# Hybrid decoder block: load order at the ways into gate and up and into down, and where residual pieces and the last weighting stand

## Chip, cores, metric

One core of a Trainium2 chip. The metric is the device time of one execution in microseconds, the median of three runs.

## The reference

The input is `x`, 2048 tokens of 1024 features in float32. The block computes:

```
u    = rmsnorm(x, ln1_g)
proj = u @ w_in                      # a_q a_f a_i a_g (512 columns each), b_q 512, b_k 128, b_v 128
y_a  = hgrn2_mixer(...)              # gated linear recurrence, 4 heads, chunks of 64 tokens
y_b  = swa_sink_attention(...)       # 8 query heads on 2 key heads, window 128, sinks, ALiBi
h    = x + concat(y_a, y_b) @ w_out
u    = rmsnorm(h, ln2_g)
h    = h + (silu(u @ w_gate) * (u @ w_up)) @ w_down      # 1024 -> 2816 -> 1024
out  = rmsnorm(h, final_g)
```

## The kernel before

Every product is made in three matmuls: each operand is split into a high part that TensorE multiplies in its reduced float32 form (made by ScalarE as a copy) and the remainder (made by VectorE as a subtraction), and high × high, high × remainder and remainder × high are added up in PSUM.

The tokens are worked in four blocks of 512. A first phase (`slots` and `out_b`, called for each block `it`) makes the input projection, both mixers and the output projection. The FFN then runs over two pairs of blocks, `p` = 0 and 1: `ffn(p)` makes gate and up, `down(p)` the last product. Both use a scheme with seven block products in place of eight. Its operands on the token side are named B11, B21, T2, T1, T3, B22, T4 (L69); T1 to T4 are differences that VectorE makes with `combine`, the B's are plain. Each is loaded by `load_operand` in four pieces of 256 KB from `u_scr`, split by `op_hi` (ScalarE) and `op_lo` (VectorE, 128 x 2048). The products of one weight group `g` run in the order A11, A12, S2, S1, S3, S4, A22 with the operands B11, B21, T2, T1, T3, B22, T4. Weights of a group come as two halves of 512 KB (`load_ffn`), four of the seven factors are sums that GpSimd makes in `ffn_sums`, and `ffn_hi`/`ffn_lo` split them.

`down(p)` runs over 77 rows `rr` = 11 `q` + `j`. A row is one 256-row slice step: a weight half row and an activation tile, 256 KB each, loaded by `load_row` into one of four ring places (`rr` mod 4), split by `row_hi` and `row_lo` (128 x 1024), and used by 12 matmuls for four token tiles. `load_row(rr)` waits until row `rr` - 4 is done (`s_row`); rows 1 to 3 of a pair wait for other things since their ring places share memory with buffers of `ffn`. For each of the seven `q`, VectorE adds the finished banks to the residual tiles `res` (`residual(p, q - 1, j)`, at `j` = 0 to 3 of the next `q`). The residual itself is loaded from `ht_scr` piece by piece by `load_res`; the list `PIECES` and the dictionary `pieces` in SP's `down` say behind which row's load each piece is issued. VectorE's loop in `down` is: for each `rr`, `row_lo(rr + 2)`, then the additions, then the final norm's steps.

All engines work through an order that is written out by hand; semaphores do the rest. SP issues all DMAs, so that a load whose semaphore is not met holds back all later ones. What the change and the prediction touch:

- SP: `mixers` (L807 and on, the last block's branch), the order of stores and loads in `ffn` (L848 and on), `load_row` (L730), `load_res` (L758), the dictionary `pieces` in `down` (L898 and on).
- ScalarE: `out_b` and `ffn`, the places of `op_hi(0, T4)` and `op_hi(0, B22)`; `out_square` makes the sums of squares for the final norm.
- VectorE: `residual` (L2269), `last_gain` (L2293: the right half of the last pair's second block times `final_g`, ahead of the norm factor), `out_scale`, `down`.

A load of the first weights waits in `load_ffn` for `s_group` at `NSB * UNITS - 2`, since the buffer shares memory with a weight unit of the output projection. The addition that opens the first block product waits for all its pieces at once:

```
if q in BEGINS + (2, 6) and q != 1 and b == 0:
    dve.wait_ge(s_ht[m ^ half], 128 * p + 64 * (m + 1))
```

where every piece adds 16 to its semaphore, and BEGINS is (0, 1, 3).

Of the kernel before, what the change touches and what calls it, by code (L numbers as in the profile page):

```python
# [42 lines left out]
TB = T // P  # L43
# [36 lines left out]
A11, A12, S2, S1, S3, S4, A22 = range(PRODUCTS)  # L80
B11, B21, T2, T1, T3, B22, T4 = range(PRODUCTS)
# [12 lines left out]
PIECES = (("r", 0), "T3", "T1", ("r", 2), "T2", ("r", 1), "T4", "B11", "B21", "B22", ("r", 3))  # L94
COMBINE_AT = {27: 0, 37: 1, 39: 2, 48: 3}
SPLIT_AT = {50: "B11", 52: "T2", 54: "T1", 59: "T3", 61: "B21", 63: "T4", 65: "B22"}
T_LOAD = 9
U_LAST = ((5, 6), (6, 3), (6, 6), (7, 3))

# [36 lines left out]
def block_program(nc, x, ln1_g, w_in, lb_logits, hgrn_norm_g, attn_sinks, attn_norm_g, w_out, ln2_g,  # L136
# [14 lines left out]
    NPAIR = NSB // 2  # L151
    NJ = KF // 2
# [22 lines left out]
    with ExitStack() as ctx:  # L175
# [325 lines left out]
        s_sst = sem("s_sst")  # L501
# [87 lines left out]
        def _(sp):  # L589
# [140 lines left out]
            def load_row(p, rr):  # L730

                q, j = divmod(rr, NJ)
                if rr >= CRING:
                    sp.wait_ge(s_row, p * NR + rr - CRING + 1)
                elif rr == 0 and p == 0:
                    wait_u_stored(sp, NSB - 1)
                elif rr == 1:
                    sp.wait_ge(s_flo, NQ * (p + 1))
                elif rr == 2:
                    sp.wait_ge(s_blk, 3 * NG * (p + 1))  # L740
                    sp.wait_ge(s_u, (NSB - 1) * TB + 2 * TB)
                elif rr == 3:
                    sp.wait_ge(s_c21[1], NJ * (p + 1))
                    sp.wait_ge(s_sst, 48 * (NJ * (p + 1) - 1))
                ring = RING[rr % CRING][2]
                combined, k, half = WEIGHT_HALF[q]
                if combined:
                    sp.wait_ge(s_ts, 16 * NJ)
                sp.dma_start(ring[:, 0, :], (t_scr if combined else w_down_k)[2 * j + k, :, half * T:(half + 1) * T]
                             ).then_inc(s_ring[rr % CRING], 16)  # L750
                done = p * NJ + (j + 1 if q == 0 else NJ)
                if q in (0, 1, 4, 6):
                    sp.wait_ge(s_ast[{0: 0, 1: 3, 4: 2, 6: 1}[q]], 16 * done)
                else:
                    sp.wait_ge(s_sst, 48 * done)
                sp.dma_start(ring[:, 1, :], a_scr[p, q, j, :, :]).then_inc(s_ring[rr % CRING], 16)
# [50 lines left out]
            def mixers(it):  # L807
                last = it + 1 == NSB
                for n in range(2, IN_GROUPS):
                    load_split(it, n)  # L810
                    if n < 2 + TB:
                        store_h(it - 1, n - 2)
                    if n == G2_LOAD:
                        load_g2(it)
                    if n == X_LOAD and not last:
                        for b in range(2):
                            sp.wait_ge(s_ptr0, (it + 1) * 2 * TB)
                            load_x(it + 1, b, x_next[b])
                    if n == X_LOAD_2 and not last:
                        for b in range(2, TB):  # L820
                            sp.wait_ge(s_u, it * TB)
                            load_x(it + 1, b, x_next[b])
                    if n == X_LOAD and last:
                        for b in range(2):
                            load_rows(it, b)
                for n in range(OUT_A, OUT_B):
                    if n > OUT_A:
                        store_u(it - 1, n - OUT_A - 1)
                    if last and n != OUT_A + 1:
                        load_operand(0, {OUT_A: T3, OUT_A + 2: T1, OUT_A + 3: T2}[n])  # L830
                    load_split(it, n)
                for c in range(4):
                    for what, n in ((("u", 3), ("r", 0), ("r", 1), ("u", 4)), (("u", 5), ("r", 2), ("u", 6)),
                                    (("u", 7), ("r", 3)), ())[c]:
                        if what == "u":
                            store_u(it - 1, n)
                        elif not last or n >= 2:
                            load_rows(it, n)
                    load_split(it, OUT_B + c)
                    if last:  # L840
                        load_operand(0, (B11, B21, T4, B22)[c])
                if last:
                    load_ffn(0, 0)
                else:
                    load_split(it + 1, 0)
                    load_split(it + 1, 1)

            def ffn(p):  # L848
# [5 lines left out]
                for g in range(NG):  # L854
# [11 lines left out]
                    if g % 2 == 0:  # L866
                        if 0 < g < NG - 2:
                            load_ffn(p, g + 2)
                        if p == 0 and 0 <= g - T_LOAD < NJ:
                            load_t(g - T_LOAD)  # L870
                    else:
                        last = j == NJ - 1
                        store_a(p, j, 0)
                        if last:
                            load_row(p, 0)
                        else:
                            load_ffn(p, g + 2)
                        if p == 0 and 0 <= g - T_LOAD < NJ:
                            load_t(g - T_LOAD)
                        if last:  # L880
                            load_row(p, 1)
                        store_a(p, j, 1)
                        if last:
                            load_row(p, 2)
                            load_row(p, 3)
                        store_s(p, j, 0)
                        store_s(p, j, 1)
                        if last:
                            load_row(p, 4)
                        store_a(p, j, 2)  # L890
                        store_a(p, j, 3)
                        store_s(p, j, 2)
# [5 lines left out]
            def down(p):  # L898
                pieces = {}
                for i in range(TB * len(PIECES)):  # L900
                    pieces[(6, 7, 8, 10)[i] if i < TB else 4 + i * 29 // 20] = (PIECES[i // TB], i % TB)
                assert len(pieces) == TB * len(PIECES)
                for rr in range(CRING + 1, NR):
                    load_row(p, rr)
# [435 lines left out]
        def _(act):  # L1340
# [221 lines left out]
            def out_b(it):  # L1562
# [31 lines left out]

                if not following:
                    ffn_hi(0, 1)
                    ffn_hi(0, 2)


# [43 lines left out]
            def ffn(p):  # L1643
                for g in range(NG):
                    G, j = NG * p + g, NJ * p + g // 2
                    x, y, z = banks_of(p, g)
                    for o in range(PRODUCTS):
# [27 lines left out]
                                    act.wait_ge(s_sst, 48 * j)  # L1675
                                A(gq[3][:, :], x[:, :], ACT.Silu).then_inc(s_c21[0], 1)
                        if p == 0 and g == 0 and o == A11:
                            op_hi(0, T4)
                        if p == 0 and g == 0 and o == A12:
                            op_hi(0, B22)  # L1680
                        if p == 0 and g in (1, 2) and o in (S1, S4):
                            h_square(NSB - 1, 2 * g - 2 + (o == S4))
# [103 lines left out]
        def _(dve):  # L1786
# [518 lines left out]
            def down(p):  # L2305
                for rr in range(NR):
# [2 lines left out]
                        row_lo(p, rr + 2)  # L2309
                    if q and j < TB:  # L2310
                        residual(p, q - 1, j)
                    if p + 1 == NPAIR and q == 6 and TB <= j < 2 * TB:
                        last_gain(p, j - TB)
                    if q == 6 and j == TB + 1:
                        out_sums(p, 0)
                    if q == 6 and j == TB + 2:
# [236 lines left out]
```

## Time and profile before

| | us |
|---|---|
| median of three runs | 2177.64 (2177.31 to 2179.43) |
| the profiled execution, device time | 2177.87 |
| its span | 2175.8 |
| TensorE matmul busy | 2151.5 (99%) |
| VectorE busy | 1309.5 (60%) |
| ScalarE busy | 892.6 (41%) |
| GpSimd busy | 444.1 (20%) |
| 16 DMA engines, share of the span | 53.9% |

The page gives the busy time of each engine, a strip of 40 slices of the span with the clock granted to TensorE, and groups of instructions with the idle time ahead of them and what ended it. A wait matters where it is TensorE that waits. The timeline shows single instructions: start, duration, engine, line, output and inputs, and in brackets the idle time before and what ended it.

In the trace of before, the first phase ends and `ffn(0)` begins near 894 us, `down(0)` near 1322, `ffn(1)` near 1535, `down(1)` near 1954; the last row is done near 2166.

### The profile page before, as it was taken

What the parts mean: (1) busy time and instruction counts of PE and PEld (TensorE: products, weight loads), DVE (VectorE), ACT (ScalarE), POOL (GpSimd) and SP (SyncE); (2) the same over time, 40 slices, a digit from 0 to 9 for tenths busy, and PEclk for the clock granted to TensorE, in tenths of its full rate; (3) what the DMA queues carried; (4) which work ended last, traced back from release to release, by engine and by line L of the source; (5) the groups of instructions that cost most, each with busy time, mean ns of one, the idle gap of its engine ahead of it and who ended that gap; (6) DMA issues with size and microseconds to landing.
All of it is one profiled execution on the core that took longest, in us unless ns stands there. A gap on an engine that the chain in (4) does not pass through costs nothing.

```text
span 2175.8 us, 29163 instructions
## 1 busy us (share of the span) xinstructions
PE 2151.5 (99%) x10836; PEld 1792.6 (82%) x10836; DVE 1309.5 (60%) x2046; ACT 892.6 (41%) x1692; POOL 444.1 (20%) x393
## 2 busy tenths in 40 slices
PE   8999999999999999999999999999999999999998
PEld 7888888888888888788888887888888888887886
DVE  5776466446644665666576765567755556554556
ACT  5543443334332433444333333346433333333444
POOL 2331023102310231322332230001232233210000
PEclk9999999999999999999999999999999999999999
DMA  7665744664466437543265556787432323237666
GB/s 244 228 254 204 261 165 155 195 217 166 154 198 223 165 136 231 214 139 127 98 217 208 209 202 227 260 271 249 170 106 102 105 89 121 92 99 245 223 208 222
DMA packets 215740, 402.49 MB, mean 185 GB/s; under 512 B 16944, under 2 KB 100912, under 8 KB 211760
## 3 DMA queue, kind: packets, MB, share of 16 engines
q1 hardware_dynamic: 215600, 400.63, 53.9%
q8 instruction: 87, 1.43, 0.3%
q14 instruction: 53, 0.43, 0.1%
HBM read 292.04 MB, written 108.53 MB: 184 GB/s over the span
## 4 chain that ended last, share of the span: by engine, by line
PE 93%; DVE 3%; DMA 2%; ACT 1%; issue 1%; SPq 1%; POOL 0%; DVEq 0%; ACTq 0%; POOLq 0%
PE M L1268 10%; PE M L1269 10%; PE M L1270 10%; PE M L960 7%; PE M L962 7%; PE M L961 7%; PE M L1293 3%; PE M L1294 3%; PE M L1295 3%; PE X L1270 3%; PE X L1269 3%; PE X L1268 3%; PE X L1294 3%; PE X L1295 3%; PE X L1293 3%; PE M L1085 2%
## 5 line engine op out<-in xcount | busy, mean ns | idle before, releaser
L2267 DVE TENSOR_TENSOR ring_lo<-ring_raw,ring_hi 128x1024 fp32r<-128x1024 f32 x154 | 189.6, 1231 | 165.3 <-ACT ring_hi L1701 164.8
L1701 ACT ACTIVATE ring_hi<-ring_raw 128x1024 fp32r<-128x1024 f32 x154 | 163.2, 1060 | 231.6 <-DMA ring_raw<-a_scr 228.3
L1268 PE MATMUL M<-t_hi,wu_hi 128*128 128x512 f32 x616 | 240.2, 390 | 0.2
L1270 PE MATMUL M<-t_hi,wu_lo 128*128 128x512 f32 x616 | 239.9, 390 | 0.0
L1269 PE MATMUL M<-t_lo,wu_hi 128*128 128x512 f32 x616 | 239.7, 389 | 0.0
L960 PE MATMUL M<-uhi,split 128*128 128x512 f32 (+1 forms) x528 | 207.7, 393 | 2.9 <-DVE ulo L1837 2.9
L962 PE MATMUL M<-uhi,split 128*128 128x512 f32 (+1 forms) x528 | 202.8, 384 | 0.0
L961 PE MATMUL M<-ulo,split 128*128 128x512 f32 (+1 forms) x528 | 202.4, 383 | 0.0
L2153 DVE TENSOR_TENSOR wu_lo<-fraw,wu_hi 128x512 fp32r<-128x512 f32 x132 | 123.3, 942 | 122.5 <-ACT wu_hi L1641 122.2
L2447 POOL TENSOR_TENSOR pr<-pr,rd 128x512 f32<-128x512 f32 x64 | 73.2, 1143 | 454.1 <-DVE rd L1848 454.1
L2516 POOL TENSOR_TENSOR fs<-fraw 128x512 f32<-128x512 f32 x44 | 62.7, 1424 | 446.0 <-DMA fraw<-in_w_gate_dram 209.0
L1268 PEld LDWEIGHTS M<-t_hi,wu_hi 128*128 128x128 f32 x616 | 115.6, 188 | 25.0 <-DVE wu_lo L2153 1.0
L1269 PEld LDWEIGHTS M<-t_lo,wu_hi 128*128 128x128 f32 x616 | 115.8, 188 | 23.9
L1270 PEld LDWEIGHTS M<-t_hi,wu_lo 128*128 128x128 f32 x616 | 115.6, 188 | 24.1
L2522 POOL TENSOR_TENSOR fraw<-fraw,fs 128x512 f32<-128x512 f32 x44 | 57.1, 1297 | 369.5 <-DVE wl_lo L2153 369.4
L1293 PE MATMUL M<-ring_hi 128*128 128x512 f32 x308 | 121.0, 393 | 3.2 <-DVE ring_lo L2267 3.2
L1294 PE MATMUL M<-ring_lo,ring_hi 128*128 128x512 f32 x308 | 119.9, 389 | 0.0
L1295 PE MATMUL M<-ring_hi,ring_lo 128*128 128x512 f32 x308 | 119.9, 389 | 0.0
L1293 PE MATMUL X<-ring_hi 128*128 128x512 f32 x308 | 119.9, 389 | 0.0
L1295 PE MATMUL X<-ring_hi,ring_lo 128*128 128x512 f32 x308 | 119.8, 389 | 0.0
L1294 PE MATMUL X<-ring_lo,ring_hi 128*128 128x512 f32 x308 | 119.8, 389 | 0.0
L960 PEld LDWEIGHTS M<-uhi,split 128*128 128x128 f32 x528 | 99.2, 188 | 25.0 <-issue 6.5
(301 smaller groups left out, 5024.6 us busy)
## 6 DMA issues: line engine op xcount, KB each, us to landing
split<-w_scr SPq DMA_DIRECT2D x60, 1024.0 KB, 5.4
ring_raw<-a_scr SPq DMA_DIRECT2D x154, 256.0 KB, 3.6
w_scr<-split SPq DMA_DIRECT2D x30, 1024.0 KB, 6.3
split_next<-w_scr SPq DMA_DIRECT2D x30, 1024.0 KB, 5.5
fraw<-in_w_gate_dram SPq DMA_DIRECT2D x44, 512.0 KB, 4.8
fraw<-in_w_up_dram SPq DMA_DIRECT2D x44, 512.0 KB, 4.8
a_scr<-au SPq DMA_DIRECT2D x88, 256.0 KB, 2.4
ring_raw<-t_scr SPq DMA_DIRECT2D x88, 256.0 KB, 3.0
```

Source lines behind the costliest of these rows:

```text
L960: mm(bank, whi[s][:, kb, :], hi, start=first, stop=False)
L961: mm(bank, whi[s][:, kb, :], lo, start=False, stop=False)
L962: return mm(bank, wlo[s][:, kb, :], hi, start=False, stop=last)
L1268: mm(bank[:, :], wh[:, k, :], hi[:, k, :], start=start and k == 0, stop=False, skip_group_check=True)
L1269: mm(bank[:, :], wh[:, k, :], lo[:, k, :], start=False, stop=False, skip_group_check=True)
L1270: last = mm(bank[:, :], wl[:, k, :], hi[:, k, :], start=False, stop=k == KH - 1, skip_group_check=True)
L1293: mm(bank[:, :], hi[:, 1, tokens], hi[:, 0, :], start=first, stop=False, skip_group_check=True)
L1294: mm(bank[:, :], hi[:, 1, tokens], lo[:, 0, :], start=False, stop=False, skip_group_check=True)
L1295: done = mm(bank[:, :], lo[:, 1, tokens], hi[:, 0, :], start=False, stop=last, skip_group_check=True)
L1701: A(hi[:, :, :], raw_r[:, :, :], ACT.Copy).then_inc(s_rowhi, 1)
L2153: V.tensor_tensor(wl[:, :, :], ffn_part(g, o), wh[:, :, :].bitcast(F32), ALU.subtract).then_inc(s_flo, 1)
L2267: V.tensor_tensor(lo[:, :, :], raw_r[:, :, :], hi[:, :, :].bitcast(F32), ALU.subtract).then_inc(s_rowlo, 1)
```

## The change

The list of edits: on SP, B22's load moves behind the first gate weights. On ScalarE, T4's high part moves ahead of the third weight of the first group, and B22's into the place where T4's stood. In SP's `ffn`, the load of row 3 moves behind the first two stores of sums of the last block, and its wait on `s_sst` goes. The four pieces of the first residual part, which were issued behind rows 6, 7, 8 and 10, are issued behind rows 8, 10, 13 and 16, in both pairs. The four `last_gain` steps move from rows 70, 71, 72, 73 to rows 63, 64, 65 and 70.

```
@@
+GAIN_AT = (63, 64, 65, 70)
@@ load_row (SP)
                 elif rr == 3:
                     sp.wait_ge(s_c21[1], NJ * (p + 1))
-                    sp.wait_ge(s_sst, 48 * (NJ * (p + 1) - 1))
@@ mixers (SP)
                     load_split(it, OUT_B + c)
-                    if last:
-                        load_operand(0, (B11, B21, T4, B22)[c])
+                    if last and c < 3:
+                        load_operand(0, (B11, B21, T4)[c])
                 if last:
                     load_ffn(0, 0)
+                    load_operand(0, B22)
@@ ffn (SP)
                         if last:
                             load_row(p, 2)
-                            load_row(p, 3)
                         store_s(p, j, 0)
                         store_s(p, j, 1)
                         if last:
+                            load_row(p, 3)
                             load_row(p, 4)
@@ down (SP)
-                    pieces[(6, 7, 8, 10)[i] if i < TB else 4 + i * 29 // 20] = (PIECES[i // TB], i % TB)
+                    pieces[(8, 10, 13, 16)[i] if i < TB else 4 + i * 29 // 20] = (PIECES[i // TB], i % TB)
@@ out_b (ScalarE)
                     ffn_hi(0, 1)
+                    op_hi(0, T4)
                     ffn_hi(0, 2)
@@ ffn (ScalarE)
                         if p == 0 and g == 0 and o == A11:
-                            op_hi(0, T4)
-                        if p == 0 and g == 0 and o == A12:
                             op_hi(0, B22)
@@ down (VectorE)
-                    if p + 1 == NPAIR and q == 6 and TB <= j < 2 * TB:
-                        last_gain(p, j - TB)
+                    if p + 1 == NPAIR and rr in GAIN_AT:
+                        last_gain(p, GAIN_AT.index(rr))
```

## Rows read from the trace of the kernel before

**Rows 1.** The page: busy time by engine, and TensorE's granted clock by slice.

```profile
PE 2151.5 (99%) x10836; PEld 1792.6 (82%) x10836; DVE 1309.5 (60%) x2046; ACT 892.6 (41%) x1692; POOL 444.1 (20%) x393
...
PEclk9999999999999999999999999999999999999999
```

**Rows 2.** Timeline of TensorE, way into gate and up, rows with idle time (start, duration).

```profile
894.73 0.50 PE L1268 MATMUL M<-b_hi,wl_hi 128*128 128x512 f32 x1 [0.60 <-DVE wl_lo L2153]
...
899.81 0.50 PE L1268 MATMUL M<-b_hi,wl_hi 128*128 128x512 f32 x1 [2.03 <-DVE wl_lo L2153]
...
912.68 0.50 PE L1268 MATMUL M<-b_hi,wu_hi 128*128 128x512 f32 x1 [0.85 <-DVE wu_lo L2153]
```

**Rows 3.** Timeline of TensorE, rows 4 and 5 of down, pair 0 and 1.

```profile
1334.21 0.50 PE L1293 MATMUL M<-ring_hi 128*128 128x512 f32 x1 [0.27 <-DVE ring_lo L2267]
...
1337.56 0.50 PE L1293 MATMUL M<-ring_hi 128*128 128x512 f32 x1 [0.33 <-DVE ring_lo L2267]
...
1965.85 0.50 PE L1293 MATMUL M<-ring_hi 128*128 128x512 f32 x1 [0.51 <-DVE ring_lo L2267]
...
1969.18 0.50 PE L1293 MATMUL M<-ring_hi 128*128 128x512 f32 x1 [0.32 <-DVE ring_lo L2267]
```

**Rows 4.** Timeline of the last rows: row 76 on ScalarE, VectorE and TensorE.

```profile
2158.58 1.06 ACT L1701 ACTIVATE ring_hi<-ring_raw 128x1024 fp32r<-128x1024 f32 x1 [1.94 <-DMA ring_raw<-a_scr]
...
2159.00 0.69 DVE L2297 TENSOR_TENSOR res<-res,gfrow 128x512 f32<-128x512 f32 x1
...
2160.80 1.22 DVE L2267 TENSOR_TENSOR ring_lo<-ring_raw,ring_hi 128x1024 fp32r<-128x1024 f32 x1
...
2162.07 0.50 PE L1293 MATMUL M<-ring_hi 128*128 128x512 f32 x1 [0.64 <-DVE ring_lo L2267]
```

**Rows 5.** Timeline near row 14 of down, pair 0, then row 16's load of pair 1.

```profile
1359.67 0.33 SPq L749 DMA_DIRECT2D ring_raw<-in_w_down_dram  x1
...
1362.20 0.39 PE L1293 MATMUL M<-ring_hi 128*128 128x512 f32 x1
...
1362.39 0.33 SPq L749 DMA_DIRECT2D ring_raw<-in_w_down_dram  x1
...
1363.85 1.06 ACT L1701 ACTIVATE ring_hi<-ring_raw 128x1024 fp32r<-128x1024 f32 x1 [1.43 <-DMA ring_raw<-a_scr]
...
1991.29 0.33 SPq L749 DMA_DIRECT2D ring_raw<-in_w_down_dram  x1
...
1994.62 1.06 ACT L1701 ACTIVATE ring_hi<-ring_raw 128x1024 fp32r<-128x1024 f32 x1 [1.57 <-DMA ring_raw<-a_scr]
```

**Rows 6.** Timeline of SP: B22's four pieces, and the first gate weights.

```profile
878.57 1.87 SPq L701 DMA_DIRECT2D b_raw<-u_scr  x4
...
883.25 0.94 SPq L671 DMA_DIRECT2D fraw<-in_w_gate_dram  x2
```

**Rows 7.** A window ahead of the first weights' landing: busy by engine, clock, DMA share, GB/s.

```profile
886.00:888.00 2.00, 2.00 (x10) 1.66 (x9) 1.90 (x2) 0.00 (x0) 0.00 (x0) 1.00 1.04 404
```

**Rows 8.** Timeline of ScalarE, VectorE and GpSimd, way into gate and up.

```profile
893.31 0.63 ACT L1641 ACTIVATE wl_hi<-fraw 128x512 fp32r<-128x512 f32 x1 [11.16 <-DMA fraw<-in_w_gate_dram]
...
895.79 2.29 DVE L2144 TENSOR_TENSOR t_lo<-t_raw,t_hi 128x2048 fp32r<-128x2048 f32 x1 [1.12 <-ACT t_hi L1616]
...
898.00 1.75 DVE L2153 TENSOR_TENSOR wl_lo<-fraw,wl_hi 128x512 fp32r<-128x512 f32 x1
...
902.07 1.36 DVE L2153 TENSOR_TENSOR wu_lo<-fs,wu_hi 128x512 fp32r<-128x512 f32 x2
...
908.65 3.38 DVE L2144 TENSOR_TENSOR b_lo<-b_raw,b_hi 128x2048 fp32r<-128x2048 f32 x1
...
894.27 1.55 POOL L2516 TENSOR_TENSOR fs<-fraw 128x512 f32<-128x512 f32 x1 [34.02 <-PE X L970]
```

**Rows 9.** Timeline of SP, way into down, pair 0: loads of rows 4 and 5.

```profile
1326.08 0.47 SPq L749 DMA_DIRECT2D ring_raw<-in_w_down_dram  x1
...
1329.26 1.13 SPq L749 DMA_DIRECT2D ring_raw<-in_w_down_dram  x1
```

More of the change, by code:

```diff
@@ L96 @@
 SPLIT_AT = {50: "B11", 52: "T2", 54: "T1", 59: "T3", 61: "B21", 63: "T4", 65: "B22"}
+GAIN_AT = (63, 64, 65, 70)
 T_LOAD = 9
@@ L743, in load_row @@
                     sp.wait_ge(s_c21[1], NJ * (p + 1))
-                    sp.wait_ge(s_sst, 48 * (NJ * (p + 1) - 1))
                 ring = RING[rr % CRING][2]
@@ L839, in mixers @@
                     load_split(it, OUT_B + c)
-                    if last:
-                        load_operand(0, (B11, B21, T4, B22)[c])
+                    if last and c < 3:
+                        load_operand(0, (B11, B21, T4)[c])
                 if last:
                     load_ffn(0, 0)
+                    load_operand(0, B22)
                 else:
@@ L884, in ffn @@
                             load_row(p, 2)
-                            load_row(p, 3)
                         store_s(p, j, 0)
@@ L888, in ffn @@
                         if last:
+                            load_row(p, 3)
                             load_row(p, 4)
@@ L900, in down @@
                 for i in range(TB * len(PIECES)):
-                    pieces[(6, 7, 8, 10)[i] if i < TB else 4 + i * 29 // 20] = (PIECES[i // TB], i % TB)
+                    pieces[(8, 10, 13, 16)[i] if i < TB else 4 + i * 29 // 20] = (PIECES[i // TB], i % TB)
                 assert len(pieces) == TB * len(PIECES)
@@ L1596, in out_b @@
                     ffn_hi(0, 1)
+                    op_hi(0, T4)
                     ffn_hi(0, 2)
@@ L1677, in ffn @@
                         if p == 0 and g == 0 and o == A11:
-                            op_hi(0, T4)
-                        if p == 0 and g == 0 and o == A12:
                             op_hi(0, B22)
@@ L2311, in down @@
                         residual(p, q - 1, j)
-                    if p + 1 == NPAIR and q == 6 and TB <= j < 2 * TB:
-                        last_gain(p, j - TB)
+                    if p + 1 == NPAIR and rr in GAIN_AT:
+                        last_gain(p, GAIN_AT.index(rr))
                     if q == 6 and j == TB + 1:
```

## The prediction

> **What bounds the kernel now.** I read the page first. TensorE is busy 99% of the span and its granted clock is full everywhere [rows 1], so a part of the change counts only where TensorE starts a matmul late, or makes it start one late. Next I read TensorE's own line of the timeline for idle time at the three places that the diff touches. At the way into gate and up it is idle 0.60, 2.03 and 0.85 us, always for a weight remainder made by VectorE [rows 2]. At the way into down, two rows of each pair wait for their remainder: 0.27 and 0.33 us in pair 0, 0.51 and 0.32 in pair 1 [rows 3]; the row before each of them waits too, but its load is released by the product of the last block (`s_c21`), which the change leaves alone. At the end the last row waits 0.64 us [rows 4]. A matmul after such a wait takes 0.50 us where the stream goes on every 0.23 (the pitch of a row, below, by 12), so I add 0.27 to each gap. One row of down is 12 matmuls; by SP's loads, one released per finished row, it is 2.72 us (1359.67 to 1362.39) [rows 5].
>
> The profiled execution took 2177.87 us with a span of 2175.8; its sum is made there and moved to the median, 2177.64.
>
> **Way into gate and up.** SP issues the four pieces of B22 (1 MB) at 878.57 and the first gate weights at 883.25 [rows 6]. The weights wait for `s_group` before and after, so they are not issued earlier; what goes is 1 MB ahead of them in a queue that moves 404 GB/s [rows 7]: 2.6 us. ScalarE sat idle 11.16 us for them and began at 893.31 [rows 8]; now 890.7. From there, engine by engine: T3's high part to 893.2, its remainder on VectorE (2.29 us [rows 8]) to 895.5. GpSimd cannot start before TensorE's last output product, 894.27, and it and VectorE take turns: a weight remainder, 0.68 each at 902.07, took 1.75 at 898.00 beside a GpSimd sum, and b_lo took 3.38 beside another, 1.1 over the 2.29 of its kind [rows 8]. So a sum of about 1.2 blocks VectorE and the other way round, and whoever waited first goes first. GpSimd's first sum now runs 895.5 to 896.7, the second weight remainder ends at 897.3 (TensorE wants it at 896.7, and had it at 899.8), the second sum ends at 898.5, its high part at 899.1, the four `h` additions at 899.7, the remainders for S2 and S1 at 900.3 and 900.9. Before, the same pair ended at 903.43 (902.07 + 1.36) [rows 8]: 2.5 us. T4's high part, now before the third weight, fills ScalarE's wait for GpSimd; B22's, 1.9 us, follows the fourth weight, with its data landed long before (1 MB behind the weights, by 893.3). From 903.43 to the remainder for S4 at 912.6 VectorE and GpSimd were a closed chain: T4 and B22 remainders, two weights, one addition, GpSimd sums between. ScalarE was a little late in it, but that time went to a sum of GpSimd that must now run anyway. So S4 starts 2.5 us sooner, and a gap of about 1.3 us is left before it. I take **2.5 saved**. Bounds: all three gaps with their refill, 0.60 + 2.03 + 0.85 + 0.81 = 4.3; 0 if the weights land no sooner.
> The Trainium skill, page "SBUF — State Buffer", section "SBUF: two separate sides", calls the port pair of VectorE and GpSimd an exclusive lock that the later one waits out. The stretched rows agree with it; if the two only shared bandwidth, S4's remainder would be ready before TensorE and this part would give about 3.8.
>
> **Way into down.** The wait of the fourth row (row 3) on `s_sst` was met long before, since those stores belong to earlier blocks: taking it away is worth 0. Its load still goes when `s_c21` lets it. The two stores of sums, whose data are made before that, are now issued in the time in which SP waits for it, and leave SP's queue between rows 3 and 4. Row 4's load went at 1326.08 [rows 9] and its products began at 1334.21 [rows 3], 8.1 us later. Its ring place is free when row 0 is done, 1325.2 (counted back from row 4 by 2.72 each and the gaps): ready at 1333.3, where TensorE wants it at 1333.7. Row 5's went at 1329.26 [rows 9], 8.3 before its products; with SP free it goes when row 1 is done, about 1327.9: ready at 1336.2 against 1336.4. Both gaps go, if only just: 0.27 + 0.33 + 2 × 0.27 = 1.14 in pair 0, 0.51 + 0.32 + 0.54 = 1.37 in pair 1: **2.5 saved** (1.5 to 2.5). Next late is row 3, as before, and its stores' data, now ahead of its load in the queue, may cost it some tenths.
>
> **Residual pieces.** They leave rows 6, 7, 8 and 10, worth 0, since the rows behind them weren't late after row 5. But they land later, and somebody waits: VectorE's `residual(p, 0, 0)` stands in its loop at row 11, behind `row_lo` of row 13, and waits for `s_ht` at 64, that is for all four pieces. The fourth is now issued behind the load of row 16, which waits until row 12 is done. Behind that waiting addition stands the remainder of row 14. TensorE has row 13 to do, 2.72 us, and then nothing. In pair 0: row 16's loads begin at 1359.67 and ScalarE takes the row at 1363.85 [rows 5]. The piece is issued 0.5 us behind them in the same queue; 256 KB at 404 GB/s is 0.65, so it lands at 1364.5. Then the addition (0.69 for such a shape [rows 4], the next starts 0.60 after it did), the remainder (1.23) and twice 0.05 to start: TensorE has row 14 at 1366.4 instead of 1362.20 [rows 5], 4.2 us idle, 4.5 with refill. In pair 1 row 16 is issued at 1991.29 and taken at 1994.62 [rows 5]; row 14 was due 2.53 after the issue as in pair 0, at 1993.8, and comes at 1994.62 + 0.65 + 1.93 = 1997.2: 3.4, with refill 3.65. After it VectorE needs 1.83 us per row against 2.72 and is ahead again. **8.1 lost**. Bounds: the piece lands with the row ahead of it (1.3 less for both), or takes 1.5 us longer each (3 more).
>
> **Last weighting.** Three of the four multiplications by `gfrow` (0.69 at 2159.00 [rows 4]) move to rows 63 to 65, where VectorE idles between remainders and the squares that they wait for follow at once; the gain row itself is loaded at row 45. In the last rows ScalarE's high part of row 76 is ready at 2159.64 but VectorE reaches it at 2160.80 [rows 4]: 1.16 late, after two multiplications. It can start at 2159.7 to 2160.9 in the new order (two or three 0.6 us steps less in the chain of rows 74 to 76), before TensorE wants it. The gap goes: 0.64 + 0.27 = **0.9 saved** (0.6 to 1.1: the additions behind the last row gain what VectorE gains, at most 1.1).
>
> **Sum:** 8.1 − 2.5 − 2.5 − 0.9 = +2.2 us. Profiled execution 2180.1, span 2178.0; median 2179.9. With the bounds: 8.1 − 1.3 less 4.3 + 2.5 + 1.1 is −1.1, and 11.1 less 0 + 1.5 + 0.6 is +9.0.
>
> **Rivals.** (A) *The clock falls in the new idle time, and the kernel is slower.* Place: row 14 of down in both pairs, the only idle times above the 2.03 us that the trace of before shows near full clock. Point: if the granted clock goes to its 1.2 GHz level at the end of a stall, a row of down takes 5.44 instead of 2.72. One row so in one pair gives +2.7, in both +5.4: 2182.6 to 2185.3. For it: 4.2 and 3.4 us of nothing on TensorE; against: no gap of before moved the clock [rows 1], and none was as long, so the trace can't exclude it. 0.18. The Trainium skill, page "TensorE: Matmul & The Clock Gate", section "HAM oscillation — how this bites in real kernels", says that TensorE waiting on DMA between bursts falls to half clock; by it this rival could come true in either pair. No row of before shows such a fall.
> (B) *The first weights land no sooner*, because B22's pieces, issued right behind them, share the 16 engines with them, or because it was `s_group` all along. Then the 2.5 us of the entry are missing: +4.7, 2182.3. Against: landings at this place follow the order of issue at the full 404 GB/s. 0.10.
> (C) *The stall isn't there*: the addition is covered, say because rows of down run behind and the piece lands in time. Then −5.9: 2171.7, faster. Against: the order by semaphores leaves no way round it. 0.04.
> (D) *Everything at its good end*: −1.1, 2176.5. 0.08.
> The forecast has 0.60.
>
> **Numbers.** About 0.2%, 4.4 us, is what a measurement of this kernel can tell from no change: below 2173.3 is faster, above 2182.0 slower. Faster: C, 0.05. Slower: A, half of B, and the forecast's upper bounds (a longer landing of the piece, fewer gaps closed), in all 0.27. Same: 0.68. The range leaves out C and the far ends: 2176.3 to 2185.5.
>
> **What would show it.** Right: in both pairs an idle time of 3 to 5 us on TensorE before row 14 of down, released by VectorE's remainder, which follows an addition to `res` that waited for a DMA from `ht_scr`; rows 4 and 5 without a gap; the first `wl_hi` about 2.6 us sooner after the last output product; one gap of about a microsecond before S4; no gap before the last row. Wrong: no wait at row 14 (the sum falls to −5.9), a granted clock below 1.00 in the slices of down (rival A), the first `wl_hi` still 11 us after ScalarE's last piece of work (rival B).

## The result, and the profile after

The changed kernel takes 2185.49 us (2183.42 to 2186.48), the kernel before, timed beside it, 2177.61: ratio 1.0032, interval 1.0022 to 1.0042. It is 7.9 us slower. The forecast was 2179.9, no change that can be measured, with a range up to 2185.5. By the prediction's own mark (above 2182.0) that is slower, to which it gave 0.27. The range, whose upper end takes in rival A at its full price (2185.3), just held the result, with some luck: the entry fell short and a disturbance of one execution came on top. The likeliest case, to which no change belonged, did not come. What came out is the forecast's mechanism with rival A on top of it, in both pairs.

The profiled execution took 2186.16 us with a span of 2184.1, against 2177.87 and 2175.8 before. The page's engine rows (busy time, share, instructions) show no more work on TensorE than before, to be read against [rows 1]:

```profile
PE 2154.2 (99%) x10836; PEld 1795.8 (82%) x10836; DVE 1311.0 (60%) x2046; ACT 892.6 (41%) x1692; POOL 445.4 (20%) x393
```

In the table of waits (total us, times, longest) TensorE's row for the remainder of a row of down has grown, from the first line (before) to the second (changed): half as many waits, three times the time.

```profile
PE M L1293 <- DVE ring_lo L2267: 3.2, 8, 0.6
...
PE M L1294 <- DVE ring_lo L2267: 9.5, 4, 4.6
```

TensorE's timeline of the changed kernel at the diff's places answers to [rows 2], [rows 3] and [rows 5]:

```profile
897.69 0.50 PE L1269 MATMUL M<-b_hi,wl_hi 128*128 128x512 f32 x1 [0.60 <-DVE wl_lo L2153]
911.26 0.50 PE L1269 MATMUL M<-b_hi,wu_hi 128*128 128x512 f32 x1 [1.96 <-DVE wu_lo L2153]
...
1329.63 0.50 PE L1294 MATMUL M<-ring_hi 128*128 128x512 f32 x1 [0.57 <-DVE ring_lo L2267]
...
1364.49 0.50 PE L1294 MATMUL M<-ring_hi 128*128 128x512 f32 x1 [4.64 <-DVE ring_lo L2267]
1365.53 0.63 PE L1294 MATMUL X<-ring_hi 128*128 128x512 f32 x1
1365.95 0.63 PE L1295 MATMUL X<-ring_lo,ring_hi 128*128 128x512 f32 x1
...
2000.63 0.79 PE L1294 MATMUL M<-ring_hi 128*128 128x512 f32 x1 [3.42 <-DVE ring_lo L2267]
```

At row 14 TensorE is idle 4.64 us in pair 0 and 3.42 in pair 1. Behind the first of them matmuls follow each other every 0.42 us instead of 0.23. The windows show why; columns are stretch, length, busy time and count of TensorE, its weight loads, VectorE, ScalarE and GpSimd, then the granted clock, DMA share and GB/s. First after, then the same stretches before:

```profile
1360.00:1365.00 5.00, 0.51 (x2) 0.47 (x3) 2.39 (x4) 2.34 (x3) 0.00 (x0) 1.00 0.68 236
1365.00:1368.00 3.00, 3.00 (x8) 2.35 (x8) 3.00 (x5) 0.32 (x1) 0.00 (x0) 0.50 0.00 0
2001.00:2006.00 5.00, 5.00 (x13) 3.84 (x13) 4.77 (x6) 0.76 (x1) 0.00 (x0) 0.50 0.00 0
```

```profile
1365.00:1368.00 3.00, 3.00 (x15) 2.49 (x14) 2.71 (x3) 1.06 (x1) 0.00 (x0) 1.00 0.80 268
2001.00:2006.00 5.00, 5.00 (x24) 4.14 (x23) 2.45 (x2) 1.09 (x2) 0.00 (x0) 1.00 0.60 195
```

Half the clock, half the matmuls in a stretch that is busy to the end: 13 in place of 24. A share of busy time of 99% hides that, and so does the page's strip of 40 slices, 54 us each: its row of granted clocks reads 9 everywhere, as before, and only the mean of the whole span shows it, 0.996 against 0.999. The strip of [rows 1], by which the prediction called the clock full everywhere, could not have shown a fall of this length either, and its own sign for rival A, a granted clock below 1.00 in the slices of down, would have missed this one. The windows do show it.

The stall is the one that the prediction describes. The chain of work of the changed kernel (start, duration) runs through the fourth residual piece in both pairs, and VectorE's timeline shows the addition that waited for it and the remainder of row 14 behind it:

```profile
1358.01 4.57 DMA res<-ht_scr
...
1995.37 3.36 DMA res<-ht_scr
```

```profile
1362.61 0.69 DVE L2280 TENSOR_TENSOR res<-res,M 128x512 f32<-128x512 f32 x1 [6.93 <-DMA res<-ht_scr]
1363.21 1.22 DVE L2267 TENSOR_TENSOR ring_lo<-ring_raw,ring_hi 128x1024 fp32r<-128x1024 f32 x1
```

**Ledger.** I took one event at a time and compared its start in the two traces; the running difference is after minus before.

| event | before | after | difference | this step |
|---|---|---|---|---|
| S4's product starts | 912.68 | 911.26 | −1.42 | entry −1.42 |
| row 16's load, pair 0 | 1359.67 | 1357.16 | −2.51 | rows 3 to 5, −1.09 |
| row 19's load, pair 0 | 1367.83 | 1371.88 | +4.05 | +6.56: 4.64 + 0.27 idle, 1.65 clock |
| up's load, `ffn(1)` | 1547.19 | 1552.18 | +4.99 | +0.94, unforeseen |
| row 0's load, pair 1 | 1941.94 | 1946.94 | +5.00 | 0 |
| row 16's load, pair 1 | 1991.29 | 1994.51 | +3.22 | rows 3 to 5, −1.78 |
| row 19's load, pair 1 | 1999.45 | 2009.20 | +9.75 | +6.53: 3.42 + 0.27 idle, 2.84 clock |
| last row's load | 2154.66 | 2164.24 | +9.58 | −0.17 |
| last matmul | 2166.06 | 2174.70 | +8.64 | last weighting −0.94 |
| end of the span | | | +8.3 | behind it −0.3 |

The clock is what is left of the 6.56 and 6.53 when the idle time and its refill are taken off: 1.65 + 2.84 = 4.5 us. The shorter stall has the dearer clock: the low level lasts 3.4 us in pair 0 (1365.0 to 1368.4) and 6.8 in pair 1 (1999.9 to 2006.7), of which the first 0.8 are still idle.

```profile
1999.90:2006.60 6.70, 5.97 (x14) 4.72 (x15) 5.87 (x7) 1.06 (x1) 0.00 (x0) 0.50 0.02 6
```

The first line of the ledger counts from the start of the span. The last matmul of the first phase began at 893.73 before and at 893.98 in the changed kernel, so that of S4's 1.42 us the entry itself gained 1.67, and 0.25 were lost ahead of it.

### The profile page after: what moved, and what is told of

The parts are those of the page before. It is cut to its first block, busy times and chain, and to the rows that moved or that the text cites. A ratio compares the mean times of both kernels' runs of the same rounds, so it can differ in the third digit from the quotient of the medians.

```text
span 2184.1 us, 29161 instructions
## 1 busy us (share of the span) xinstructions
PE 2154.2 (99%) x10836; PEld 1795.8 (82%) x10836; DVE 1311.0 (60%) x2046; ACT 892.6 (41%) x1692; POOL 445.4 (20%) x393
## 4 chain that ended last, share of the span: by engine, by line
PE 93%; DVE 3%; DMA 2%; ACT 1%; issue 1%; SPq 0%; POOL 0%; ACTq 0%; DVEq 0%; POOLq 0%
PE M L1271 10%; PE M L1269 10%; PE M L1270 10%; PE M L961 7%; PE M L963 7%; PE M L962 7%; PE M L1294 3%; PE X L1294 3%; PE X L1296 3%; PE M L1296 3%; PE M L1295 3%; PE X L1295 3%; PE X L1271 3%; PE X L1270 3%; PE X L1269 3%; PE M L1086 1%
```

## Experiments

Medians, ratios to the kernel before and their intervals; e7 and e11 were timed once.

| kernel | us | ratio |
|---|---|---|
| e1 changed, pieces back | 2174.05 (2172.27 to 2176.38) | 0.9984 (0.9975 to 0.9992) |
| e2 before, pieces moved | 2190.15 (2190.09 to 2190.73) | 1.0058 (1.0044 to 1.0071) |
| e3 changed, 11 idle products | 2181.56 (2180.02 to 2184.08) | 1.0018 (1.0009 to 1.0027) |
| e4 changed, additions late | 2173.24 (2172.05 to 2175.00) | 0.9979 (0.9970 to 0.9988) |
| e5 before, entry | 2178.03 (2176.70 to 2179.76) | 0.9999 (0.9988 to 1.0009) |
| e6 before, rows | 2176.08 (2175.43 to 2177.17) | 0.9990 (0.9980 to 1.0000) |
| e7 before, B22's load alone | 2178.03 | one execution |
| e8 changed, 15 idle products | 2182.37 (2179.94 to 2183.05) | 1.0016 (1.0007 to 1.0026) |
| e9 changed, pieces 6, 7, 8, 16 | 2186.13 (2185.04 to 2188.20) | 1.0038 (1.0025 to 1.0051) |
| e10 changed, pieces 6, 7, 8, 13 | 2174.75 (2173.04 to 2176.32) | 0.9983 (0.9973 to 0.9993) |
| e11 before, weighting alone | 2178.97 | one execution |
| e12 e4 and B22 ahead of T4 | 2172.43 (2170.46 to 2173.33) | 0.9972 (0.9961 to 0.9984) |

**e1: take the residual pieces back.** In the changed kernel:

```
-pieces[(8, 10, 13, 16)[i] if i < TB else ...
+pieces[(6, 7, 8, 10)[i] if i < TB else ...
```

> The changed kernel with the four residual pieces back behind rows 6, 7, 8 and 10. Theory (VectorE waits for the fourth piece, TensorE runs dry before row 14, and its clock falls on top): both stalls go with the clock's part, 6.56 us in pair 0 and 6.53 in pair 1, so 13.1 less than the changed kernel and about 4.8 less than before: 2172.8. Rival (the pieces are innocent, the loss comes from the new order of stores and loads at the way into down or at the entry): no more than a microsecond off the changed kernel, 2184 to 2185.

It took 2174.05, 11.4 us below the changed kernel, where 2172.8 and 13.1 were expected; a likely part of what is missing is told in the last section. No wait at row 14 is left, the clock of the whole span is 0.999, and the table of waits has only row 3:

```profile
PE M L1294 <- DVE ring_lo L2267: 0.6, 1, 0.6
```

The rest of the change, then, is worth 3.4 us of gain against before in these runs, and the pieces alone turn it into a loss.

**e2: move only the pieces**, in the kernel before.

```
-pieces[(6, 7, 8, 10)[i] if i < TB else ...
+pieces[(8, 10, 13, 16)[i] if i < TB else ...
```

> The kernel before with only the four residual pieces moved to rows 8, 10, 13 and 16. Theory: both stalls with the fall of the clock, +13 us: 2190.6 (2188 to 2193), TensorE idle 4.6 and 3.4 us before row 14. Rival (the pieces need the other edits, which let rows run ahead, to become late): under +3 us, 2178 to 2181.

2190.15 us, 12.7 us above the kernel before, which took 2177.43 beside it. Its timeline of TensorE has the stalls and nothing else of the change, though row 5 waited 1.25 us in this execution:

```profile
1368.00 0.80 PE L1293 MATMUL M<-ring_hi 128*128 128x512 f32 x1 [4.39 <-DVE ring_lo L2267]
...
2004.46 0.79 PE L1293 MATMUL M<-ring_hi 128*128 128x512 f32 x1 [4.15 <-DVE ring_lo L2267]
```

The clock fell both times. By the loads of rows 16 and 19, as in the ledger, 6.06 us are lost in pair 0 (1360.92 to 1375.14, where three rows of 2.72 are 8.16) and 6.64 in pair 1 (1997.62 to 2012.42), 12.7 together. In the ledger it was 13.1. Without the idle time (4.39 and 4.15) and the refill the clock is 1.4 and 2.2 of it. The change alone and its undoing agree.

**e3: keep the stall, keep TensorE at work.** Eleven small products in front of row 14, in both pairs, into one of the banks of `down`.

```
+                    if rr == 14:
+                        for _ in range(11):
+                            mm(down_banks(p, 1)[0][:, 0:P], ones[:, :], ones[:, :], start=False, stop=False,
+                               skip_group_check=True)
```

> The changed kernel, and TensorE makes 11 small products of a constant tile before row 14 in both pairs, in the time in which it waits; they are added into one bank, so that part of the output isn't the reference's. Theory (part of the loss is the clock, which falls because TensorE is idle): row 14 starts as late as before, but the granted clock stays full and 4.5 us of the loss go: 2181. Rival (the clock falls for another reason, or TensorE is slow after the wait for want of data): no gain, 2185 to 2186, granted clock again 0.50 for some microseconds.

2181.56, 3.9 us below the changed kernel, as expected in size (2181). The products are added into a bank that is in use, so the output is wrong; only the time counts here. The trace is less simple. TensorE's timeline:

```profile
1359.45 2.62 PE L1307 MATMUL M<-ones 128*128 128x128 f32 x22
1364.06 0.55 PE L1294 MATMUL M<-ring_hi 128*128 128x512 f32 x1 [1.99 <-DVE ring_lo L2271]
...
1995.05 2.62 PE L1307 MATMUL M<-ones 128*128 128x128 f32 x22
1998.77 0.50 PE L1294 MATMUL M<-ring_hi 128*128 128x512 f32 x1 [1.10 <-DVE ring_lo L2271]
```

and its windows behind the two places:

```profile
1365.00:1368.00 3.00, 3.00 (x9) 2.34 (x8) 3.00 (x5) 0.40 (x1) 0.00 (x0) 0.54 0.00 0
...
1999.00:2005.00 6.00, 6.00 (x27) 4.94 (x27) 4.92 (x6) 0.85 (x1) 0.00 (x0) 1.00 0.26 90
```

After 1.10 us of idle time the clock stayed, and pair 1 lost 3.87 us in place of 6.53. After 1.99 it fell, and pair 0 lost 6.33. The filler was too short in pair 0.

**e8: the same with 15 products.**

```
-                        for _ in range(11):
+                        for _ in range(15):
```

> As the kernel with 11 small products in TensorE's wait, but with 15 (3.6 us where 11 took 2.6), so that about 1.0 us of idle time is left before row 14 in pair 0 and about 0.1 in pair 1; they are added into one bank, so that part of the output isn't the reference's. Theory (the clock follows how much TensorE does): granted clock full after both waits, each pair loses only what row 14 is late, 4.9 and 3.7, and the total is 2180.5 to 2181. Rival (in pair 0 the clock falls for something else than idle time): it falls again to 0.50 there, 2181.5 to 2182.5.

Now the idle time left is 0.76 and 0.31 us, and the clock is full behind both:

```profile
1364.00:1370.00 6.00, 5.48 (x24) 4.58 (x25) 5.67 (x7) 1.06 (x1) 0.00 (x0) 1.00 0.26 93
...
1999.00:2005.00 6.00, 6.00 (x27) 4.99 (x28) 5.01 (x6) 1.06 (x1) 0.00 (x0) 1.00 0.25 87
```

By the loads of rows 16 and 19, 4.38 and 3.93 us are lost, 8.3 against 13.1 in the changed kernel: the 4.8 between them is the clock, in these two traces, and the 8.3 is the wait itself, forecast as 8.1. The medians give less: 2182.37 was expected at 2180.5 to 2181, is only 3.1 us below the changed kernel, and is no lower than e3's; the intervals of the two overlap. In the profiled execution of e8 row 3 of down waited 1.11 us in pair 0 and 0.30 in pair 1, against 0.57 and 0.11 in the changed kernel, 0.7 us more and up to 1.1 with a refill; whether that holds for the other executions is not known, and so the rest of the 4.8 stays open.

**e4: take away what makes VectorE wait**, with SP's new order kept. The first additions to `res` go from `j` = 0 to 3 of `q` = 1 to `j` = 4 to 7:

```
-                    if q and j < TB:
+                    if q > 1 and j < TB:
                         residual(p, q - 1, j)
+                    if q == 1 and TB <= j < 2 * TB:
+                        residual(p, 0, j - TB)
```

> The changed kernel with the pieces where the change puts them (rows 8, 10, 13, 16), but VectorE makes the four additions of the first block product at rows 15 to 18 and not at 11 to 14. Theory (what costs is that VectorE waits in order, ahead of row 14's remainder): no stall, 2172.8 as with the pieces put back. Rival (the transfers themselves, at rows 13 and 16, push row loads back): the loss stays for the most part, 2180 or more.

2173.24, 12.3 below the changed kernel, no wait at row 14. Expected was 2172.8. So the late pieces do nothing to TensorE but through VectorE's order.

**e9 and e10: how late may the fourth piece be?** The changed kernel with pieces behind rows 6, 7, 8 and 16 (e9) or 6, 7, 8 and 13 (e10; the two new lines below in this order).

```
-pieces[(8, 10, 13, 16)[i] if i < TB else ...
+pieces[(6, 7, 8, 16)[i] if i < TB else ...
+pieces[(6, 7, 8, 13)[i] if i < TB else ...
```

> The changed kernel with three residual pieces back behind rows 6, 7 and 8 and only the fourth left behind row 16. Theory (the addition waits for the count of all four, so the last alone decides): TensorE idle 4.6 and 3.4 us before row 14 as in the changed kernel, 2184 to 2186. Rival (each late piece adds its part, or the load of DMAs at rows 8 to 13 is the cost): less than half of the loss, under 2180.

> The changed kernel with the pieces behind rows 6, 7, 8 and 13: the fourth three rows sooner than the change has it, three later than before. Theory: it is issued when row 9 is done and lands about when row 13 does, which is when VectorE reaches the addition anyway; no idle time at row 14, 2172.5 to 2174. Rival (the cost grows with each row that the piece is later): about half of the loss, 2178 to 2180.

e9 is as slow as the changed kernel, 2186.13, with gaps of 4.38 and 3.42 us at row 14. Here the low level lasted 6.8 us in pair 0 and 3.4 in pair 1, the other way round than in the changed kernel; pair 1 lost 5.23 us behind the same gap that cost 6.53 there. e10 takes 2174.75, 0.75 above what was expected, and has no gap at row 14: its addition goes without a wait.

```profile
1358.91 0.68 DVE L2280 TENSOR_TENSOR res<-res,M 128x512 f32<-128x512 f32 x1
```

Where the first three pieces stand makes no difference (e9); the fourth costs nothing at row 13 and everything at row 16.

**e5 and e7: the way into gate and up alone**, in the kernel before: all of it (e5), and only B22's load behind the gate weights, ScalarE's order as before (e7; the last line below is e5's alone, and there B22's split takes T4's old place).

```
-                    if last:
-                        load_operand(0, (B11, B21, T4, B22)[c])
+                    if last and c < 3:
+                        load_operand(0, (B11, B21, T4)[c])
                 if last:
                     load_ffn(0, 0)
+                    load_operand(0, B22)
...
                     ffn_hi(0, 1)
+                    op_hi(0, T4)
```

> The kernel before with only the edits at the way into gate and up (B22's load behind the first weights, T4's and B22's high parts moved on ScalarE). Theory (the forecast's chain of VectorE and GpSimd, as the changed kernel's trace sized it): the S4 product starts 1.4 us sooner than before, near 911.3, with 1.9 us of idle time ahead of it, and the total falls by 1.4, 2176.2. Rival (the forecast's own size): 2.5 sooner, 2175.1.

> The kernel before with only B22's load behind the first gate weights; ScalarE's order as before. Theory (the weights' landing is worth A11 and A12, and T4's place on ScalarE is worth little since GpSimd's sums fill the time): first weights 2.1 to 2.6 us sooner, S4 near 911.3 to 911.8. Rival (T4's place is what shortens the chain to S4): S4 at 912.5, as before, with more idle time ahead of it.

e5 took 2178.03: no gain, ratio 0.9999, where 2176.2 was expected. Its trace shows the gain and the giving back, in the timeline of TensorE and the window behind it:

```profile
911.31 0.50 PE L1269 MATMUL M<-b_hi,wu_hi 128*128 128x512 f32 x1 [1.92 <-DVE wu_lo L2153]
```

```profile
912.00:916.00 4.00, 4.00 (x13) 3.10 (x12) 1.06 (x2) 0.00 (x0) 0.00 (x0) 0.57 0.64 199
```

S4 starts 1.37 us sooner than before's 912.68; then 13 matmuls run where the changed kernel has 19 in the same stretch at full clock, and a store that leaves at 926.40 before leaves at 926.64 here and at 924.98 in the changed kernel: about 1.6 us given back. In e7 the first split starts almost as soon as in the changed kernel, and S4 at 911.62:

```profile
891.37 0.63 ACT L1642 ACTIVATE wl_hi<-fraw 128x512 fp32r<-128x512 f32 x1 [8.67 <-DMA fraw<-in_w_gate_dram]
```

The end of the first phase moves by up to 0.8 us between executions, so I count S4 from the start of the last output matmul: 18.92 to 18.95 us in the four kernels without the entry edit (before, e2, e6, e11), 17.40 in e7, 17.22 to 17.28 in seven of the eight kernels that have all of it and VectorE's order as it was (16.80 in e3). The transfer's place in the queue is worth 1.5 of the 1.7, the places of T4 and B22 on ScalarE 0.15, each from one execution.

Does a fall at the old place, before A12, cost as much? The clock fell there in e6 and e11:

```profile
901.50:904.80 3.30, 3.30 (x9) 2.60 (x8) 2.37 (x4) 3.30 (x4) 2.01 (x2) 0.50 0.00 0
```

and still S4 came 18.92 and 18.95 us behind the last output matmul, and the store 32.6 and 32.7, as in before and e2, where it did not fall. S4 waits for VectorE there, and the slower matmuls ran in time that TensorE would have waited: the gaps of 0.12 and 0.85 us that before has between A12 and S4 are absent in both. The entry edit joins the idle time into one gap with no such wait behind it: with a fall the store leaves 32.6 to 32.8 us behind the last output matmul (e5, e7, e10), without one at 31.0 (e3 30.5). A fall takes back all but 0.1 of what the edit gains.

**e6: the way into down alone**, in the kernel before.

```
-                    sp.wait_ge(s_sst, 48 * (NJ * (p + 1) - 1))
...
                             load_row(p, 2)
-                            load_row(p, 3)
                         store_s(p, j, 0)
                         store_s(p, j, 1)
                         if last:
+                            load_row(p, 3)
                             load_row(p, 4)
```

> The kernel before with only the stores ahead of row 3 and without its wait on the older stores. Theory: rows 4 and 5 of down start without a gap in both pairs, 1.1 us saved in pair 0 and 1.4 to 1.8 in pair 1: total 2174.9. Rival (the gain there needs the pieces out of rows 6 to 10): under 1 us, with a gap left before row 4 or 5.

2176.08, 1.9 us below before where 2.9 was expected. Rows 4 and 5 wait no more in either pair, but the row in front of them does, longer than ever:

```profile
1332.64 0.50 PE L1292 MATMUL M<-ring_hi 128*128 128x512 f32 x1 [1.73 <-DVE ring_lo L2266]
```

Row 3's gap in pair 0 is 0.15 to 0.45 us in the five kernels without this edit (before, e2, e5, e7, e11). With it there are 0.57, 0.62, 0.76, 1.47, 1.73, 1.11, 0.70 and 1.33 (the changed kernel, e1, e3, e4, e6, e8, e12, e10), and none in e9. The stores ahead of its load are what this edit changes for it, so I put the 0.2 to 1.3 us more in most executions down to them; the two weren't tried one by one. The gaps of rows 3 to 5 in pair 0 add up to 1.02 us in before, but to 1.28 to 1.83 in e2, e5, e7 and e11, where the loads are in the same order: before's profile shows them at their smallest.

**e11: the last weighting alone**, in the kernel before, timed once.

```
-                    if p + 1 == NPAIR and q == 6 and TB <= j < 2 * TB:
-                        last_gain(p, j - TB)
+                    if p + 1 == NPAIR and rr in GAIN_AT:
+                        last_gain(p, GAIN_AT.index(rr))
```

> The kernel before with only the four multiplications by the gain row moved to rows 63, 64, 65 and 70. Theory: VectorE reaches row 76 a microsecond sooner, TensorE has no gap before the last row, the stretch from SP's last row load to the last matmul is 0.9 us shorter than in the kernel before. Rival (another step of VectorE takes the place of the multiplications): the gap stays at 0.3 us or more.

From the last row's load to the last matmul it took 11.09 us, against 11.40 before and 10.46 in the changed kernel. Half the gap stayed (0.31 in place of 0.64), because row 73's data came late and ScalarE waited 2.71 us for them. That is one execution with a disturbance of its own; it neither supports nor refutes the 0.9. The eight other kernels with this edit took 10.46 us (e4 10.63), the five without it 11.01 to 11.47 (e5 and e7 11.01 and 11.11, with the weighting as before). So the edit goes with 0.4 to 1.0 us less, but it never gave that by itself.

**e12: close the new gap before S4.** e4, and VectorE splits B22 ahead of T4:

```
-                        if p == 0 and g == 0 and o == A11:
-                            op_lo(0, T4)
-                        if p == 0 and g == 0 and o == A12:
+                        if p == 0 and g == 0 and o == A11:
                             op_lo(0, B22)
+                        if p == 0 and g == 0 and o == S2:
+                            op_lo(0, T4)
```

TensorE's wait on `s_oplo` counts in that order.

> The kernel with the late additions, and VectorE makes B22's remainder ahead of T4's in the first group (B22 after the fourth weight's remainder, T4 after the sixth). Theory (the 1.96 us ahead of S4 are VectorE and GpSimd working through T4, which only the product after S4 needs): the gap before S4 goes, no new one before A22, 2.2 us less than with the late additions alone: 2171.0. Rival (the chain is as long as TensorE's products, so the gap moves to A22): 2172.5 to 2173.2.

The 1.92 us in front of S4 are gone, 0.56 stand in front of the T4 product instead, so a part of the gap did move to A22, as the rival has it; the clock is full:

```profile
912.37 0.47 PE L1270 MATMUL M<-t_hi,wu_hi 128*128 128x512 f32 x1 [0.56 <-DVE gq L2186]
```

2172.43 is the fastest kernel of the study: by the ratios 0.28%, 6 us, below the kernel before and 0.60%, 13 us, below the changed one. Counted from the last output matmul the store leaves 1.5 us sooner than in e4. But the median is only 0.8 less than e4's, within the spread of both and nearer to the rival's 2172.5 than to the theory's 2171.0, so the last step is likely but not proven.

## Where the prediction was right, and where it was wrong

**The stall at row 14: right.** Place, cause and size came out: 4.64 us against 4.2 in pair 0, 3.42 against 3.4 in pair 1. In pair 0 the piece landed at 1362.58 (1358.01 + 4.57), 5.42 us behind the load of row 16, where the step had 4.83 (1364.5 less 1359.67 [rows 5]), 0.6 us later. e8 has the wait by itself at 8.3, forecast 8.1. e1, e2, e4, e9 and e10 leave no other cause.

**The clock: the step that failed. Rival A came true, and it had too small a chance.** The step took a stall to cost its length and a refill, and the clock behind it nothing. Rival A, with 0.18, priced the clock at +2.7 to +5.4; it cost 4.5 in the ledger, 4.8 by e8 against the changed kernel, 3.6 in e2 and 3.8 in e9. The argument against it was that no gap of before moved the clock [rows 1], and none was as long. That is absence of evidence: a stall of 3.4 us or more has no row in before at all, and the strip of slices that was read shows no fall of this length anyway. All six such stalls of the study (two each in the changed kernel, e2 and e9) were followed by a clock at its 1.2 GHz level. The Trainium skill, page "TensorE: Matmul & The Clock Gate", section "HAM oscillation — how this bites in real kernels", says that TensorE waiting on DMA between bursts drops to half clock: the six stalls agree, 3.42 to 4.64 us, in which TensorE waited for a DMA through VectorE. The rival and the forecast were the same mechanism, and should have been put together: 8.1 lost plus 2.7 to 5.4 was the likeliest case once the stall was believed.

**The entry: mechanism right, term too large.** S4 started 1.42 us sooner, 1.67 by the last output matmul, not 2.5. The first weights are split 2.14 us sooner, 2.4 by that count (forecast 2.6). What went wrong is the chain of VectorE and GpSimd. These are its rows in the changed kernel, answering to [rows 8]; the last is the remainder that S4 waits for, by itself:

```profile
894.52 2.56 POOL L2516 TENSOR_TENSOR fs<-fraw 128x512 f32<-128x512 f32 x1 [34.28 <-PE X L971]
895.85 1.78 DVE L2153 TENSOR_TENSOR wl_lo<-fraw,wl_hi 128x512 fp32r<-128x512 f32 x1
899.95 2.38 DVE L2153 TENSOR_TENSOR wu_lo<-fs,wu_hi 128x512 fp32r<-128x512 f32 x2
900.12 1.66 POOL L2522 TENSOR_TENSOR fraw<-fraw,fs 128x512 f32<-128x512 f32 x1
902.25 2.28 DVE L2144 TENSOR_TENSOR t_lo<-t_raw,t_hi 128x2048 fp32r<-128x2048 f32 x1
906.15 3.38 DVE L2144 TENSOR_TENSOR b_lo<-b_raw,b_hi 128x2048 fp32r<-128x2048 f32 x1
907.35 3.31 POOL L2519 TENSOR_TENSOR fraw<-fraw 128x512 f32<-128x512 f32 x1
909.45 1.75 DVE L2153 TENSOR_TENSOR wu_lo<-fraw,wu_hi 128x512 fp32r<-128x512 f32 x1
```

and two of the kernel before:

```profile
904.51 2.52 DVE L2144 TENSOR_TENSOR t_lo<-t_raw,t_hi 128x2048 fp32r<-128x2048 f32 x1 [1.07 <-ACT t_hi L1616]
...
911.95 0.68 DVE L2153 TENSOR_TENSOR wu_lo<-fraw,wu_hi 128x512 fp32r<-128x512 f32 x1
```

The pair of remainders for S2 and S1 took 2.38 us beside another GpSimd sum, where the step had 1.36 as before, and ended at 902.33 instead of 900.9, 1.1 sooner than before and not 2.5. Then came what the step had put at nothing: T4's high part was ready, and VectorE did not wait 1.07 us for it as before (nor did it in e7). So `t_lo` ended, and `b_lo` began, 2.50 us sooner than before (906.15 against 908.65 [rows 8]). The last 1.1 us went at the remainder for S4, 1.75 beside GpSimd's sum of 907.35, where it was 0.68 by itself. Twice a remainder met a sum that it had not met before, and one wait fell away; so the chain was 1.4 us sooner at its end and the gap before S4 is 1.96, not 1.3; that it was 2.5 sooner in its middle, as forecast, is luck. The step let each sum meet one VectorE instruction; it has to be asked again for each instruction that moves. The page "SBUF — State Buffer" of the Trainium skill, section "SBUF: two separate sides", has the two engines exclude each other: 2.38 for a pair of 0.68 each, 1.75 for one of 0.68, 3.38 for 2.29 and 3.31 on GpSimd in the same stretch agree with that.

And closing two gaps made one of about 2 us out of 0.85. In e5, e7 and e10 that new gap took the clock with it, at 1.6 us, which no term of the sum held.

**The way into down: right in sum.** 1.09 + 1.78 = 2.9 against 2.5. Rows 4 and 5 lost their gaps. In pair 0 row 3's gap grew a little (0.42 to 0.57); in pair 1 it went from 0.45 to 0.11, which nothing promised. "May cost it some tenths" was low: e6 and e4 have 1.73 and 1.47.

**The last weighting: right in sum.** 0.94 to the last matmul, another 0.3 behind it, forecast 0.9; that the edit alone does it isn't shown (e11).

**Missed: 0.94 us between row 19 of pair 0 and `ffn(1)`.** SP's timeline of the changed kernel has one issue of 2.54 us that took 0.38 before:

```profile
1443.49 2.54 SPq L917 DMA_DIRECT2D gfrow<-in_final_g_dram  x1
```

A row behind it came late, and TensorE waited 0.90 us at 1454.34, where before waits 0.23 somewhat later. The change doesn't touch this issue, and e1, e3, e4, e8, e9, e10 and e12, which carry the change at both ways in, have it at 0.38 each. So it belongs to this execution, not to the change.

The sum, then: forecast +2.2; the clock +4.5, entry +0.8, the end of the first phase +0.3, `gfrow` +0.9, stalls with refill +0.5, ways into down −0.4, the rows of pair 1 −0.2, behind the last matmul −0.3. Together +8.3, by which the span grew.

## What to carry to other kernels

A semaphore that counts several pieces makes the last piece decide, and an in-order engine hands that wait to everything queued behind it: before moving a load later, find who waits for the whole count and what stands behind that wait. A stall on a TensorE that is otherwise full has two prices, its length and the slow stretch behind it, and the second was here 0.4 to 0.6 of the first (3.6 to 4.5 us in e2, e9 and the changed kernel); count it wherever a change makes a stall longer than any in the trace. Closing several gaps of half a microsecond can gather them into one long one further on, so ask of a closed gap where its time comes back. And ask what stands behind a gap: a slow stretch ahead of another wait can be free, and the same stretch ahead of a full stream is paid for.

## What the runs showed of the hardware that I had not expected

**Gaps of about 2 us take the clock in some executions and not in others.** The idle times of TensorE between 1.92 and 2.06 us in the profiled executions, and the granted clock behind them:

| place | clock stayed | clock fell |
|---|---|---|
| before A12, without the entry edit | before 2.03, e2 2.05 | e6 2.06, e11 2.04 |
| before S4, with the entry edit | changed 1.96, e1 1.92, e3 1.96, e4 1.92, e8 1.96, e9 1.96 | e5 1.92, e7 1.96, e10 1.95 |
| before row 14 | | e3 1.99 |

Six of fourteen, with the same work around them and the same lengths on either side. What decides between the two columns isn't shown. None of the gaps of the ways in up to 1.73 us was followed by a fall, and each stall of 3.42 us or more was. The trace of before shows a gap of 2.03 us at no such price, and I took that for a rule; e11 shows a fall behind nearly the same gap at the same place, even if it cost nothing there. Behind gaps of about 2 us the low level lasted 3.4 us each time, behind the six stalls 3.4 us three times and 6.8 three times, whatever their length; what is lost is half of the part in which TensorE has work. This also limits what one profile can say here: part of the spread of some 3 us between executions of one kernel is likely such falls. The mean clock of every execution, to three digits, fits that: in the nine kernels with the entry edit that were timed more than once, the executions with the lower clock took 0.3 to 2.0 us longer on average (e1's eight at 0.998 2174.7, its three at 0.999 2172.7, the forecast of e1), in the three sets of before −0.1 to 0.2, in e6 −0.4.

**One load, seven landings.** The changed kernel, e1, e3, e4, e8, e9 and e10 are the same program up to row 3 of pair 0, and its gap was 0.57, 0.62, 0.76, 1.47, 1.11, 0 and 1.33 us: a load with stores ahead of it in SP's queue came late by very different amounts. And one issue of a small load, `gfrow`, held SP for 2.54 us in the changed kernel, for 1.05 in e11 and for 0.38 in the twelve others.
